# Candidate positions turned into key indices by 256-element compares and predicated copies, with the low halves of the expert weights spread between them

## The reference, cut to what matters

```python
def peer_ffn(hn, w_q, sub_keys, u, v):
...
        q = (xb @ w_q).reshape(p, PEER_HEADS, 2, PEER_QHALF)
        sc = jnp.einsum('thpc,hpnc->thpn', q, sub_keys).astype(jnp.float32)
        s1, i1 = lax.top_k(sc[:, :, 0], PEER_TOPK)
        s2, i2 = lax.top_k(sc[:, :, 1], PEER_TOPK)
        cand = (s1[..., :, None] + s2[..., None, :]).reshape(p, PEER_HEADS, PEER_TOPK * PEER_TOPK)
        cand_idx = (i1[..., :, None] * PEER_NKEYS + i2[..., None, :]).reshape(p, PEER_HEADS, PEER_TOPK * PEER_TOPK)
        top_s, sel = lax.top_k(cand, PEER_TOPK)
        eidx = jnp.take_along_axis(cand_idx, sel, axis=-1).reshape(p, PEER_HEADS * PEER_TOPK)
        gate = jax.nn.softmax(top_s, axis=-1).reshape(p, PEER_HEADS * PEER_TOPK)
        act = jax.nn.gelu(jnp.einsum('td,ted->te', xb, u[eidx]).astype(jnp.float32), approximate=False) * gate
        return jnp.einsum('te,ted->td', act, v[eidx]).astype(xb.dtype)
```

## Time and profile before

| | us |
|---|---|
| median of three runs | 2310.0 (2309.59 to 2313.76) |
| the profiled execution, its own time | 2311.68 |
| its span, first to last instruction | 2309.5 |
| TensorE busy, matmul | 2176.6 |
| TensorE busy, weight loads | 1979.7 |
| VectorE busy | 1487.5 |
| ScalarE busy | 1176.8 |
| GpSimd busy | 542.9 |

### The profile page before, as it was taken

The page is one execution under the profiler, slowest core; times in us unless marked ns, Lnnn a source line. Parts: engine busy times, 40 slices in busy tenths (PEclk is TensorE's granted clock), DMA queues, the critical chain, the costliest instruction groups (busy, mean ns, idle before and its releaser), DMA issues.

```text
span 2309.5 us, 44209 instructions
## 1 busy us (share of the span) xinstructions
PE 2176.6 (94%) x14560; PEld 1979.7 (86%) x14560; DVE 1487.5 (64%) x2872; ACT 1176.8 (51%) x2573; POOL 542.9 (24%) x438
## 2 busy tenths in 40 slices
PE   7789899799999999999997898997999999999997
PEld 7689599799999888888786895997999998888886
DVE  4864247967777666666558642479677776666665
ACT  4631045476666555555545301454766665555554
POOL 6532007752222100000075220177422221000000
PEclk9899799999999999999998997999999999999999
DMA  5310244344444355555542102443444443555555
GB/s 216 110 56 1 73 165 164 133 166 156 145 145 145 128 188 193 197 186 198 183 180 89 56 1 92 155 176 140 161 151 145 145 147 129 197 191 191 199 185 189
DMA packets 47457, 338.76 MB, mean 147 GB/s; under 512 B 5648, under 2 KB 5776, under 8 KB 6928
## 3 DMA queue, kind: packets, MB, share of 16 engines
q1 hardware_dynamic: 47376, 337.73, 40.7%
HBM read 336.66 MB, written 1.05 MB: 146 GB/s over the span
## 4 chain that ended last, share of the span: by engine, by line
PE 81%; DVE 13%; ACT 2%; issue 1%; DMA 1%; POOL 0%; SPq 0%; DVEq 0%; PEldq 0%; ACTq 0%; POOLq 0%
PE ps L799 10%; PE ps L801 10%; PE ps L800 10%; PE ps L769 9%; PE ps L770 9%; PE ps L771 9%; PE ps L779 5%; PE ps L672 3%; PE ps L402 2%; PE ps L404 2%; PE ps L403 2%; PE ps L536 2%; PE ps L549 1%; PE ps L548 1%; DVE expert_lo L1596 1%
## 5 line engine op out<-in xcount | busy, mean ns | idle before, releaser
L769 PE MATMUL ps<-h_t_hi,expert_hi 128*128 128x256 f32 x2048 | 592.5, 289 | 31.1 <-DVE expert_lo L1596 26.6
L770 PE MATMUL ps<-h_t_lo,expert_hi 128*128 128x256 f32 x2048 | 580.1, 283 | 0.0
L771 PE MATMUL ps<-h_t_hi,expert_lo 128*128 128x256 f32 x2048 | 580.1, 283 | 0.0
L1747 POOL TENSOR_TENSOR expert_lo<-w_ring,expert_hi 128x512 fp32r<-128x512 f32 x220 | 330.7, 1511 | 812.1 <-ACT expert_hi L958 808.6
L958 ACT CAST expert_hi<-w_ring 128x512 fp32r<-128x512 f32 x512 | 309.4, 616 | 252.6 <-PE ps L771 243.5
L769 PEld LDWEIGHTS ps<-h_t_hi,expert_hi 128*128 128x128 f32 x2048 | 393.4, 192 | 34.9 <-DVE expert_lo L1596 17.3
L799 PE MATMUL ps<-expert_hi,act_hi 128*128 128x512 f32 x1024 | 400.5, 391 | 4.8 <-DVE act_lo L1604 4.8
L800 PE MATMUL ps<-expert_lo,act_hi 128*128 128x512 f32 x1024 | 400.3, 391 | 0.0
L801 PE MATMUL ps<-expert_hi,act_lo 128*128 128x512 f32 x1024 | 399.9, 391 | 0.0
L770 PEld LDWEIGHTS ps<-h_t_lo,expert_hi 128*128 128x128 f32 x2048 | 393.8, 192 | 0.0
L771 PEld LDWEIGHTS ps<-h_t_hi,expert_lo 128*128 128x128 f32 x2048 | 393.1, 192 | 0.0
(11 more groups left out here) (285 smaller groups left out, 3392.5 us busy)
## 6 DMA issues: line engine op xcount, KB each, us to landing
w_ring<-u_t SPq DMA_DIRECT2D x128, 1024.0 KB, 4.8
w_ring<-v_t SPq DMA_DIRECT2D x128, 1024.0 KB, 4.8
w_ring<-w_in SPq DMA_DIRECT2D x32, 1024.0 KB, 4.9
w_ring<-w_q SPq DMA_DIRECT2D x16, 1024.0 KB, 4.8
w_ring<-w_out SPq DMA_DIRECT2D x8, 1024.0 KB, 4.7
big<-xconst SPq DMA_DIRECT2D x2, 1666.0 KB, 9.5
w_ring<-keys SPq DMA_DIRECT2D x2, 1024.0 KB, 4.8
big<-rows SPq DMA_DIRECT2D x2, 576.0 KB, 11.3
```

What stands on the lines that cost most here:

```text
L769: pe.matmul(o, w_hi[:, c, :], HTH[:, d, :], start=d == 0, stop=False)
L770: pe.matmul(o, w_hi[:, c, :], HTL[:, d, :], start=False, stop=False)
L771: mm = pe.matmul(o, w_lo[:, c, :], HTH[:, d, :], start=False, stop=d == DC - 1)
L1747: pool.tensor_tensor(EL[:, m % 4, :], RING[:, m // 4, (m % 4) * 512:(m % 4 + 1) * 512], EH[:, m % 4, :].bitcast(F32), ALU.subtract).then_i ...
```

## The change

The picks no longer go tile by tile over 128x2048 elements. Both tiles are handled at once, 128x256 elements a step. For each row start 1 to 15 a `tensor_scalar` writes a mask (is the position at or behind it?), and a `copy_predicated` overwrites `I1F` with that row's key index where the mask holds; for rows 1 to 8 a second one does so for `ROWAT` (in row 8 and beyond each row has one entry, so the position itself is the row's start). The column's 15 masks and copies follow for `I2F`. Each mask has a place of its own (`MASKS`, 15 x 256), so that mask i + 1 stands in the list ahead of the copies of mask i, and the copies wait for all steps but that one. `I1F` and `I2F` are filled with index 0 of each row first, and `ROWAT` with zeros, in the place where `STEP1` was made. `few_lows(1)` stands at five places among these steps instead of six; the total of 20 stays.

```diff
--- before.py
+++ after.py
@@ -210,8 +210,7 @@
-        ISROW, PICKED = (big(2048).rearrange("p (u k n) -> p u k n", u=8, k=16) for _ in range(2))
-        STEP1 = IDX[:, 0:16, :]
+        MASKS = big(15 * 256).rearrange("p (m u n) -> p m u n", m=15, u=16)
@@ -1540,8 +1539,9 @@
-                dve.tensor_copy(STEP1[:, :, 0:1], x[:, :, 0, 0:1])
-                dve.tensor_tensor(STEP1[:, :, 1:16], x[:, :, 0, 1:16], x[:, :, 0, 0:15], ALU.subtract)
+                dve.tensor_copy(I1F[:, :, :], x[:, :, 0, 0:1].broadcast_to([P, 16, 16]))
+                dve.tensor_copy(I2F[:, :, :], x[:, :, 1, 0:1].broadcast_to([P, 16, 16]))
+                dve.memset(ROWAT[:, :, :], 0.0)
@@ -1564,25 +1564,44 @@
-                full = [P, 8, 16, 16]
-                for t in range(NT):
-                    us = slice(8 * t, 8 * t + 8)
-
-                    def over_rows(a):
-                        return a.unsqueeze(1).unsqueeze(1).broadcast_to(full)
-
-                    link(dve.tensor_tensor(ISROW, POSF[:, us, :].unsqueeze(3).broadcast_to(full), over_rows(ROWC[:, 0, :]), ALU.is_ge))
-                    link(dve.tensor_tensor(PICKED, ISROW, over_rows(ROWC[:, 1, :]), ALU.mult))
-                    few_lows(1)
-                    link(dve.tensor_reduce(ROWAT[:, us, :], PICKED, AX.X, ALU.add))
-                    dve.tensor_tensor(PICKED, ISROW, STEP1[:, us, :].unsqueeze(2).broadcast_to(full), ALU.mult)
-                    link(dve.tensor_tensor(COLF[:, us, :], POSF[:, us, :], ROWAT[:, us, :], ALU.subtract))
-                    few_lows(1)
-                    link(dve.tensor_reduce(I1F[:, us, :], PICKED, AX.X, ALU.add))
-                    link(dve.tensor_tensor(ISROW, COLF[:, us, :].unsqueeze(3).broadcast_to(full), over_rows(iota[:, 0:16]), ALU.is_equal))
-                    few_lows(1)
-                    link(dve.tensor_tensor(PICKED, ISROW, x[:, us, 1, :].unsqueeze(2).broadcast_to(full), ALU.mult))
-                    link(dve.tensor_reduce(I2F[:, us, :], PICKED, AX.X, ALU.add))
+                full = [P, 16, 16]
+
+                def counted(ins):
+
+                    steps[0] += 1
+                    ins.then_inc(dve_step, 1)
+
+                def all_but(n):
+
+                    dve.wait_ge(dve_step, steps[0] - n)
+
+                def take(dst, i, src):
+
+                    counted(dve.copy_predicated(dst[:, :, :], MASKS[:, i - 1, :, :].bitcast(U32), src))
+
+                for i in range(1, 17):
+                    if i < 16:
+                        counted(dve.tensor_scalar(MASKS[:, i - 1, :, :], POSF[:, :, :], float(ROW_AT[i]), None, ALU.is_ge))
+                    r = i - 1
+                    if r >= 1:
+                        all_but(1 if i < 16 else 0)
+                        take(I1F, r, x[:, :, 0, r:r + 1].broadcast_to(full))
+                        if r <= 8:
+                            take(ROWAT, r, POSF[:, :, :] if r == 8 else ROWC[:, 0, r:r + 1].unsqueeze(1).broadcast_to(full))
+                    if r in (4, 8, 13):
+                        few_lows(1)
+                counted(dve.tensor_tensor(COLF[:, :, :], POSF[:, :, :], ROWAT[:, :, :], ALU.subtract))
+                all_but(0)
+                for i in range(1, 17):
+                    if i < 16:
+                        counted(dve.tensor_scalar(MASKS[:, i - 1, :, :], COLF[:, :, :], float(i), None, ALU.is_equal))
+                    c = i - 1
+                    if c >= 1:
+                        all_but(1 if i < 16 else 0)
+                        take(I2F, c, x[:, :, 1, c:c + 1].broadcast_to(full))
+                    if c in (4, 12):
+                        few_lows(1)
+                all_but(0)
```

## The result

The changed kernel takes 2317.5 us (median of 20 runs, 2305.4 to 2326.1), the kernel before 2310.6 us (20 runs, 2301.3 to 2315.1). The ratio is 1.003, with a 95% interval of 1.0016 to 1.0044: slower by 0.3%. Forecast were 2303.7 us and faster. The profiled execution took 2313.64 us, with a span of 2311.5 us.

A forecast was written before the change was run, and what follows sets the result against it. TensorE's 26.6 us of waiting for VectorE's low halves was taken as the bound. VectorE's own 27.3 us plus 19.4 for GpSimd made 46.7 us, saving 3.1 us a layer, 6.3 in all: 2303.7 us, range 2282 to 2315.

The forecast's parts named there:

- Rival 1: In the picks, `copy_predicated` doesn't wait for GpSimd, so the list ends sooner: 2282 us; chance 0.16.
- number 17: VectorE's 17th low half since `topk` began, queued behind picks and `gates`; forecast done at 471.1 us in the first layer.
- the 19: GpSimd low halves before number 17, each said to cost VectorE 1.02 us: 19.4 us a layer.
- four halves later, at 477.0: After restarting at 471.2 us, TensorE takes VectorE's next low half at 477.0 us, against 480.12: 3.1 us a layer.
- so the list does set the pace: Among the picks, each stretch between low halves exceeds TensorE's 5.76 us (shortest 6.7), so VectorE's list decides the end.
- about 20: TensorE's total waits for VectorE's low halves, both layers, were to fall from 26.6 us to this many us.
- the clock at full speed all through: With no wait near 6.7 us left, TensorE's granted clock was not to drop; before, it read 0.50 behind that wait.
- The step on `gates`: Behind the picks, the three steps of `gates` and their waits were put at 1.5 us a layer.
- after that it doesn't stop: In the kernel before, TensorE runs without stopping once restarted at 480.12 us; it was busy 22.00 of 22 us there.
- Rival 2: The picks' small steps cost more than their rows; at 0.1 us a step, 3.8 us a layer slower: 2317.6 us; chance 0.15.
- Rival 3: No change that shows: half the extra step cost, or 22 GpSimd steps instead of 19: 2306 to 2314 us; chance 0.24.
- The rule of short steps: Each VectorE step has a fixed cost, about 0.16 us, which speaks against 69 steps in place of 18 in the picks.

The follow-up runs named there:

- e4: The changed kernel with the masks in idle PSUM banks instead of SBUF: 2298.3 us, ratio 0.995 to the kernel before.
- e11: The changed kernel run again, unedited: 2321.5 us, ratio 1.0051 to the kernel before.
- e12: The changed kernel with one semaphore step holding GpSimd back ahead of each of its low halves in trips 12 to 31: 2311.8 us.
- e16: The changed kernel with 18 semaphore steps of VectorE ahead of its first norm, shifting its later code: 2312.7 us.
- e1: The changed kernel with one more low half at the end of the picks, ahead of the wait in `gates()`: 2310.3 us.
- e6: The changed kernel with masks in PSUM and one more low half ahead of the wait in `gates()`: 2289.8 us.
- e7: The changed kernel, masks still in SBUF, with nine low halves among the picks instead of five: 2291.4 us.
- e14: e6 with one semaphore step holding GpSimd back ahead of each of its low halves in trips 12 to 31: 2279.7 us.

## Why the prediction was wrong

**Right, and of no use.** The place of the stake, VectorE as what TensorE waits for, and the prices: a compare 0.28 us (0.29 foretold), a copy 0.43 (0.47), about 1.1 us for each small step beside GpSimd, `copy_predicated` among them. Rival 1 is out by e4. From 424 us to number 17 the list takes until 469.99 + 1.52 = 471.5 us (471.1 foretold), and TensorE restarts at 471.56 us. That this came out is chance: fewer waits for GpSimd than the 19, since GpSimd stood still for 7.6 us around TensorE's first stop, and in their place 4.93 us of waiting for the exponential and 2.80 us for a high half; and trip 0 had begun 0.9 us earlier than in the kernel before. The next step of the sum, "four halves later, at 477.0", didn't come out: at half clock the four halves took 7.24 us instead of 5.76, and number 18 was taken at 478.80 us. Counted from the start of trip 0, that is 0.45 us earlier than before in the first layer and 2.3 us later in the second, where 3.1 us earlier was forecast.

**The first step that failed: "so the list does set the pace", and with it the waits of "about 20" us and "the clock at full speed all through".** No wait near 6.7 us was left, as foretold, but the stretches between low halves had been added up and held against the end alone. TensorE doesn't live off the sum; it stops at each feed that is late, and 10.8 us between numbers 11 and 12 against 5.76 is a stop of 4.57 us. Three such stops a layer, of 2.8 to 4.6 us, took the granted clock down in five places, where before the stop of 6.7 us had done it once a layer. Trips 0 to 11 take 158.2 us a layer in the mean of the eight layers with these picks that were profiled (after, e11, e12, e16), and 156.6 and 156.7 before. The forecast was 3.1 us less; it was 1.6 us more. e1, e4, e6 and e7 move or shorten these stretches without touching the form of the picks and win 4.2 to 15.9 us a layer over the changed kernel's execution.

The traces tell clock and waiting apart. The table is for trips 0 to 11, us a layer; the clock's cost is an estimate, from the time in which products ran at 0.50 of the clock and their starts, 0.21 us apart there instead of 0.12 (1578.38 and 1578.59 us in the changed kernel):

| | length | TensorE's waits | cost of the half clock | rest |
|---|---|---|---|---|
| before | 156.6 | 14.3 | 1.3 | 141.0 |
| changed, mean of the eight layers | 158.2 | 13.4 | 4.8 | 140.0 |

The waits were to fall by 3.3 us a layer (26.6 to 20 us in two layers) and fell by 1.0. The clock, for which the sum had no term, cost 3.6 us more than before.

**The step on `gates` failed with it.** Its three steps and their waits were put at 1.5 us by the row before, where the picks ended 14 us later and the exponential had been done for 3.8 us. Where a list becomes shorter, its later waits must be looked up at their new times. The prediction named no such wait; e1 shows that it costs the first layer its third stop.

**The second failure is one of sight: "after that it doesn't stop".** It didn't, but it went slower. The 20 trips behind the picks weren't in the sum at all. They hold the larger part of the loss: 5.3 us a layer where the tie is lost, 10.6 us in the profiled executions, and 5.7 us in the medians by e12, so in the timed runs the tie seems to be won at times. By medians, of the 6.9 us the tie took 5.7 and the picks' part 1.2 (2311.8 in e12 against 2310.6; against the runs of before on their own chips e12 and e16 are 1.8 and 1.7 us slower, and both intervals hold 1). The profiled trips 0 to 11 have 3.1 us for it in two layers.

Rival 2 had the sign, and with 2317.6 us the number too, but by luck: its mechanism isn't in the rows, where compares and copies left alone took no longer than foretold. Rival 3, no change that shows, is what the picks' part alone came to. The rule of short steps, weighed in the prediction, is no cause either: VectorE was busy for 40.1 us from 424 to 481 us where it had been busy for 55.0, and e6 and e14 with small steps have the shortest trips 0 to 11 of all.

Open: why "ahead" and "between" are 8 to 10 us shorter in some executions; and what happens at VectorE's 832nd record. A shift of 46 put it among the steps of trip 12, one of 64 put it ahead of them; the size of a block in the code doesn't follow from that. The Trainium skill (Runtime: NRT & Kernel Launch, "Instruction fetch mechanics") says that an engine's instructions are fetched in blocks of 256 and that crossing one is mostly hidden. The 0.35 us at one fixed record would fit such a crossing, here not hidden; that it is one wasn't shown.

## What to carry to other kernels

Compare two traces stage by stage by a count of work that is the same in both, here 32 products to a trip, and over the whole program, before explaining anything at the place of the change: equal busy time of TensorE and "no waits" hide a loop that runs 2% slower. Where two engines share a port in a loop, look for starts that coincide; a tie can decide all later trips, and one semaphore step that always lets the same engine go first was worth 6 to 10 us here. Place steps that feed a waiting engine by the time between them while the other engine uses the port too, and ahead of any wait, and move scratch to idle PSUM where VectorE and GpSimd meet in SBUF.
